# Which queue copies the kept rows of the sliding caches, and in which phases, in a four-layer decoder step

## The chip, the cores and the metric

The kernel runs on one core of one Trainium2 chip. The metric is the device time of one execution in microseconds (us). Three executions of the kernel before took 2611.56, 2619.59 and 2623.01 us; the median is 2619.59 us. The engines are TensorE (PE, with its weight loads as PEld), VectorE (DVE), ScalarE (ACT), GpSimd (POOL) and SyncE (SP), which only issues transfers. ACT and POOL can issue transfers too.

## The reference, cut to what matters

One step of a decoder runs 256 prompt tokens and 8 x 4 sample tokens through four layers: state space mixer, dilated sliding window attention, differential attention, state space mixer. Each mixer is followed by a SwiGLU network. The window layer keeps for each of 8 sequences a cache of key and value rows for three head groups (128, 512 and 1024 rows; a row has 512 floats, 2 KB). It must return each cache with the four new rows at its end:

```
keep = min(win, lb + T)
new_buf = jnp.concatenate([buf, jnp.stack([k, v], axis=2).astype(buf.dtype)], axis=1)[:, lb + T - keep:]
```

So of group 0 rows 4 to 127 are kept (124 rows, 248 KB), of group 1 rows 4 to 511 (508 rows, 1016 KB), and of group 2 all 1024 rows (2 MB), once for each of the 8 sequences. These kept rows depend on nothing that the kernel computes. They go from one tensor in device memory to another, 27.13 MB in all.

## The kernel before

Activations lie feature-major: `x` is 8 chunks of 128 features x 288 tokens. The four layers run one after the other, each as a list of phases; a phase is a block in which every engine has its own instruction list, and at its end all engines drain and meet (`L164`). An attention layer has these phases: the projection (`project`), the prompt attention, the sample attention (a loop over the 8 sequences), for the differential layer a short normalisation, and then `chain`, which holds the output projection, the gate and up projection and the down projection.

Dense layers stream their weights. SP loads a block of weights in two transfers into one of two slots `raw` (`load_block`, `L205`) once `split_lo` of the block two earlier has read the slot. ACT splits off the high part `wh` (`split_hi`, `L213`), DVE the low part `wl` (`split_lo`, `L221`), and PE runs three products per weight tile (`block_mm`, `L243` and `L248`). A down projection has 16 blocks of 128 x 1408 (384 KB and 320 KB). Two blocks make one output chunk, which DVE adds to `x` (`L440`). Then ACT, DVE and POOL prepare the chunk for the next layer: `next_act` (`L291`), `next_dve` (`L297`), `next_pool` (`L304` to `L309`). The last layer has no such preparation.

In the down projections of layers 0, 1 and 2, ACT also issues the copies of the kept rows, right behind `next_act` of each second block (`copy_rows`, `L576`): in layer 0 two for each sequence (groups 0 and 1), in layer 1 one for each sequence (the first half of group 2), in layer 2 one (the second half). That makes 32 transfers. The down projection of layer 3 has none. Nothing waits for them until the last phase, where SP waits for `copied` before the program ends.

The two prompt attention phases load no weights. SP loads the bias tables `HK` there (`sp_bias`, `L1603`: six transfers of 256 KB in the window layer, two of 768 KB in the differential layer), and later it stores the new keys and values. Before each `pe_bias` (`L1612`) PE waits for all of `HK`; its products turn the tables, ACT moves them to `BT`, and the first scores are biased with them (`L1773`, `L2200`). Everything later in the phase follows. POOL has no instruction list in these two phases.

Of the kernel before, what the change touches and what calls it, by code (L numbers as in the profile page):

```python
# [32 lines left out]
NB, T = 8, 4  # L33
# [8 lines left out]
PAST = 1024  # L42
# [16 lines left out]
HD = 64  # L59
WINDOWS = ((128, 1), (512, 4), (2048, 16))  # L60
GH = 4
# [83 lines left out]
def build_program(nc, A, O):  # L145
# [4 lines left out]
    def S(name, step=1):  # L150
        if name not in sig:
            sig[name] = Signal(nc, name, step)
        return sig[name]
# [53 lines left out]
    def split_hi(act, g, width):  # L207

        s = g % 2
        act.wait_ge(raw_loaded[s].sem, (g // 2 + 1) * 32)  # L210
        if g >= 2:
            act.wait_ge(blocks_done.sem, g - 1)
        act.activation(wts["hi"][:, s, 0:width], raw[:, s, 0:width], ACT.Copy).then_inc(hi_ready.sem, 1)  # L213
# [119 lines left out]
    def chain(layer, first, source, next_gain, nxt):  # L333
# [9 lines left out]
        with phase() as (block, sb):  # L343
# [20 lines left out]
            def width_ahead(seg, i):  # L364

                at = seg.b0 + i + 2
                for s in segs:
                    if s.b0 <= at < s.b0 + s.lin.n:
                        return s.lin.width
                return 0  # L370

            @block.sync
            def _(sp):
                for seg in segs:
                    for i in range(2 if seg is out else 0, seg.lin.n):
                        load_block(sp, seg.lin, i, seg.b0 + i)
                for i in range(2 if nxt else 0):
                    load_block(sp, nxt, i, out.b0 + total + i)

            @block.scalar  # L380
            def _(act):
                for i in range(2):
                    split_hi(act, out.b0 + i, first.width)
                for c in range(first.kk):
                    act.activation(oh[:, c, :], source(c), ACT.Copy).then_inc(src_hi.sem, src_hi.inc())
                for i in range(first.n):
                    for j in range(jj):
                        prep_act(act, i * jj + j)
                    split_hi(act, out.b0 + i + 2, width_ahead(out, i))
                rs_act(act)  # L390
                for i in range(KF):
                    split_hi(act, up.b0 + i + 2, width_ahead(up, i))
                    r = i % 2
                    act.wait_ge(gate_scaled.sem, gate_scaled.at(i + 1))
                    act.activation(sg[:, r, :], gt[:, r, :], ACT.Silu).then_inc(silu_ready.sem, silu_ready.inc())  # L395
                    act.wait_ge(gated_ready.sem, gated_ready.at(i + 1))
                    act.activation(hh[:, i, :], gh[:, r, :], ACT.Copy).then_inc(hid_hi.sem, hid_hi.inc())  # L397
                for i in range(2 * KD):
                    if i % 2 and next_gain is not None:
                        next_act(act, i // 2)  # L400
                    copy_rows(act, layer, i)
                    if width_ahead(down, i):
                        split_hi(act, down.b0 + i + 2, width_ahead(down, i))

# [152 lines left out]

    copied = S("cache_copied", 16)

    def kept_rows(layer):  # L560


        pick = lambda g, src, dst, n: (A[f"cache_swa_kv{g}"], O[f"swa_kv{g}_sample"], src, dst, n)
        return ([pick(0, T, 0, WINDOWS[0][0] - T), pick(1, T, 0, WINDOWS[1][0] - T)],
                [pick(2, 0, 0, PAST // 2)], [pick(2, PAST // 2, PAST // 2, PAST // 2)], [])[layer]

    def copy_rows(act, layer, i):

        for cache, dst, row, to, n in kept_rows(layer) if i % 2 else ():
            views = []  # L570
            for ap, at in ((cache, row), (dst, to)):
                size = ap.shape[2] * ap.shape[3] * GH * HD
                flat = ap.rearrange("l b w k h d -> (l b w k h d)")
                lo = i // 2 * size + at * 2 * GH * HD
                views.append(flat[lo:lo + n * 2 * GH * HD].rearrange("(w n) -> w n", n=2 * GH * HD))
            act.dma_start(views[1], views[0]).then_inc(copied.sem, copied.inc())  # L576

    def ffn_first(layer):
        return Linear(KF, KD, 2, gate_up(A["ffn_w_in"][layer]))
# [1059 lines left out]
    def swa(layer, nxt):  # L1639
# [11 lines left out]
        with phase() as (block, sb):  # L1651
# [9 lines left out]
            def _(sp):  # L1661
# [15 lines left out]
                        n += 1  # L1677
                sp.wait_ge(stored.sem, stored.at(n))

            def unit(u):  # L1680
                qt, hh = units[u]
                rows = slice(hh % 2 * 64, hh % 2 * 64 + 64)
                return qt, hh, rows, u % 2

            @block.tensor
            def _(pe):
# [12 lines left out]
                def scores(u):  # L1699
                    qt, hh, rows, r = unit(u)  # L1700
                    if u >= 2:
                        pe.wait_ge(sc_ready.sem, sc_ready.at(u - 1))
                    for g in range(3):
                        c = 2 * g + hh // 2
                        mm = pe.matmul(flat[:, r * 1024 + g * 256:r * 1024 + g * 256 + nk_of(qt)],
                                       X[rows, c, qt * P:(qt + 1) * P], X[rows, 6 + c, 0:nk_of(qt)],
                                       start=True, stop=True)
                    mm.then_inc(sc_done.sem, sc_done.inc())
                scores(0)
                pe.wait_ge(bias_moved.sem, bias_moved.at(6))  # L1710
                for u in range(len(units)):
                    if u + 1 < len(units):
                        scores(u + 1)
                    qt, hh, rows, r = unit(u)
                    pe.wait_ge(diag_ready.sem, diag_ready.at(2 * u + 2))
                    pe.wait_ge(p_ready.sem, p_ready.at(u + 1))
                    if u >= 1:
                        pe.wait_ge(pt_moved.sem, pt_moved.at(u))
                    for g in range(3):
                        for kt in range(qt + 1):  # L1720
                            o = 2048 + (2 * g + kt) * P
                            mm = pe.matmul(flat[:, o:o + P], Sb[:, r, g, kt * P:(kt + 1) * P], DR[:, r, :],
                                           start=True, stop=True)
                    mm.then_inc(pt_done.sem, pt_done.inc())
                    pe.wait_ge(pt_moved.sem, pt_moved.at(u + 1))
                    if u >= 2:
                        pe.wait_ge(o_moved.sem, o_moved.at(u - 1))
                    for g in range(3):
                        h = 4 * g + hh
                        for kt in range(qt + 1):  # L1730
                            mm = pe.matmul(ps[rows, 6 + r, g * P:(g + 1) * P], KV[:, kt, 1, h * HD:(h + 1) * HD],
                                           PT[:, r, 2 * g + kt, :], start=(kt == 0), stop=(kt == qt))
                    mm.then_inc(pv_done.sem, pv_done.inc())
# [322 lines left out]
    def kv_out(out):  # L2056

        return out.rearrange("l b t g m d -> (l b t) (g m d)" if len(out.shape) == 6 else
                             "l b t g n -> (l b t) (g n)")
# [13 lines left out]
    def diff(layer, nxt):  # L2073
# [13 lines left out]
        with phase() as (block, sb):  # L2087
# [7 lines left out]
            @block.sync  # L2095
            def _(sp):
                sp_bias(sp)
                sp.wait_ge(kv_moved.sem, kv_moved.at(2 * KV_C))
                for k, name in enumerate(("diff_k", "diff_v")):
                    for t in range(2):  # L2100
                        out = kv_out(O[name + "_prompt"])
                        sp.dma_start(out[t * P:(t + 1) * P], KV[:, t, k, :]).then_inc(stored.sem, stored.inc())
                    sp.dma_start(kv_out(O[name + "_sample"]), KV[0:NS, 2, k, :]).then_inc(stored.sem, stored.inc())
                sp.wait_ge(stored.sem, stored.at(6))

            def values(pe, u):
                qt, h = units[u]
                r = u % 2
                pe.wait_ge(pt_moved.sem, pt_moved.at(u + 1))
                if u >= 2:  # L2110
                    pe.wait_ge(o_moved.sem, o_moved.at(u - 1))
                for kt in range(qt + 1):
                    mm = pe.matmul(ps[:, 6 + r, 0:P], KV[:, kt, 1, h // REP * P:(h // REP + 1) * P],
                                   PT[:, r, kt * P:(kt + 1) * P], start=(kt == 0), stop=(kt == qt))
                mm.then_inc(pv_done.sem, pv_done.inc())
# [381 lines left out]
        with phase() as (block, sb):  # L2497
            act_norm, pe_norm, dve_norm, _ = norm_heads(block, sb, OT, QD_C, 0, V_DOUT, ones, P, 1.0 - LAM_INIT)
# [8 lines left out]


    kinds = (ssd, swa, diff, ssd)
    firsts = [ssd_first(0), swa_first(1), diff_first(2), ssd_first(3), None]  # L2510
    with stack:
# [85 lines left out]
```

## Time and profile before

| | |
|---|---|
| median of three executions | 2619.59 us |
| the profiled execution | 2618.41 us |
| its span, first to last instruction | 2616.6 us |
| PE busy | 2363.0 us, 90% |
| DVE, ACT, POOL busy | 1225.5, 992.4, 450.4 us |
| mean granted TensorE clock | 0.884 of full speed |

The page cuts the span into 40 slices of 65.4 us. In the lines by slices each digit is a share of a slice in tenths. The line PEclk gives the clock that was granted to TensorE, and the line DMA the mean busy share of the 16 DMA engines. A window of the trace gives the same for any stretch, in us from the span's start. A waits row names an engine's idle time by what ended it.

### The profile page before, as it was taken

The page shows a single profiled execution, that of the slowest core. Times are in us where ns is not written, and L with a number is a line of the kernel's source. Part 1 is how long each engine was busy: PE and PEld are TensorE (multiplying, and loading weights), DVE is VectorE, ACT ScalarE, POOL GpSimd, SP SyncE. Part 2 cuts the span into 40 slices and gives each one's busy share as a digit, 9 for nine tenths or more (in the row PEclk, how much of TensorE's full clock was granted, in tenths as well). Part 3 has the DMA queues.
Part 4 walks back from the last instruction along what each step waited for, and adds up shares of the span by engine and source line. Part 5 has one row for each costly group of instructions (what it writes and reads, how often), then busy time and mean ns, then how long its engine had stood idle before and what let it go on. Part 6 is the DMA issues. An engine that isn't in the chain of part 4 may idle for free. (4 is left out here: it accounts for less than half of the span.)

```text
span 2616.6 us, 38501 instructions
## 1 busy us (share of the span) xinstructions
PE 2363.0 (90%) x15187; PEld 2047.0 (78%) x15187; DVE 1225.5 (47%) x2074; ACT 992.4 (38%) x1497; POOL 450.4 (17%) x396
## 2 busy tenths in 40 slices
PE   6999997999896698999876799699988999979999
PEld 5877776999794455999874466599988877859999
DVE  5644444555433233654346433355546544445554
ACT  2534444443333111543344211444335434354442
POOL 2112120243100000442100000033310112202430
PEclk9888786999996698999995699899998878779999
DMA  5343332666750342656630445166674334225554
GB/s 159 97 118 99 101 85 73 170 167 176 258 160 23 78 113 67 177 162 200 218 113 19 170 160 194 33 174 168 182 250 133 108 100 125 75 66 159 164 152 140
DMA packets 505013, 352.44 MB, mean 135 GB/s; under 512 B 13517, under 2 KB 486367, under 8 KB 504133
## 3 DMA queue, kind: packets, MB, share of 16 engines
q1 hardware_dynamic: 503822, 323.01, 42.4%
q10 hardware_dynamic: 1024, 27.13, 2.7%
q8 instruction: 114, 1.87, 0.3%
q14 instruction: 53, 0.43, 0.1%
HBM read 326.59 MB, written 50.63 MB: 144 GB/s over the span
## 5 line engine op out<-in xcount | busy, mean ns | idle before, releaser
L243 PE MATMUL ps<-xh,wh 128*128 128x288 f32 x2368 | 676.4, 311 | 41.8 <-issue 24.9
L221 DVE TENSOR_TENSOR wl<-raw,wh 128x2048 fp32r<-128x2048 f32 (+3 forms) x241 | 503.9, 2092 | 354.7 <-ACT wh L213 350.2
L243 PE MATMUL ps<-xl,wh 128*128 128x288 f32 x2368 | 667.2, 306 | 0.0
L213 ACT ACTIVATE wh<-raw 128x2048 fp32r<-128x2048 f32 (+3 forms) x241 | 419.7, 1744 | 293.1 <-PE ps L248 183.4
L243 PEld LDWEIGHTS ps<-xh,wh 128*128 128x128 f32 x2368 | 474.9, 201 | 45.2 <-issue 41.1
L243 PEld LDWEIGHTS ps<-xl,wh 128*128 128x128 f32 x2368 | 473.8, 200 | 0.4
L248 PE MATMUL ps<-xh,wl 128*128 128x288 f32 x2368 | 340.1, 297 | 0.0
L248 PEld LDWEIGHTS ps<-xh,wl 128*128 128x128 f32 x2368 | 324.2, 189 | 0.0
L457 POOL TENSOR_TENSOR gh<-sg,ut 128x288 f32<-128x288 f32 x88 | 216.7, 2463 | 351.3 <-ACT sg L395 351.3
L243 PE MATMUL ps<-hh,wh 128*128 128x288 f32 x704 | 194.4, 301 | 17.2 <-issue 15.4
L243 PE MATMUL ps<-hl,wh 128*128 128x288 f32 x704 | 192.9, 300 | 0.0
L1466 DVE SCALAR_TENSOR_TENSOR H<-H,EA,ps 128x128 f32<-128x128 f32 x256 | 71.9, 343 | 205.2 <-PE ps L1027 205.2
L243 PE MATMUL ps<-oh,wh 128*128 128x288 f32 x400 | 114.1, 311 | 47.1 <-DVE ol L411 47.1
L1134 POOL TENSOR_TENSOR E<-E,cb 128x288 f32<-128x288 f32 x64 | 94.9, 1504 | 329.5 <-ACT E L1260 329.5
L243 PEld LDWEIGHTS ps<-hh,wh 128*128 128x128 f32 x704 | 134.2, 191 | 21.0 <-issue 17.6
L243 PEld LDWEIGHTS ps<-hl,wh 128*128 128x128 f32 x704 | 134.2, 191 | 0.0
L397 ACT ACTIVATE hh<-gh 128x288 fp32r<-128x288 f32 x88 | 39.2, 446 | 226.4 <-POOL gh L457 226.4
L243 PEld LDWEIGHTS ps<-oh,wh 128*128 128x128 f32 x400 | 80.3, 201 | 48.5 <-issue 48.5
L243 PE MATMUL ps<-ol,wh 128*128 128x288 f32 x400 | 113.3, 307 | 0.0
L291 ACT ACTIVATE xh<-x,vec 128x288 fp32r<-128x288 f32 x64 | 33.9, 535 | 201.3 <-DVE x L417 112.9
L248 PE MATMUL ps<-hh,wl 128*128 128x288 f32 x704 | 103.7, 295 | 0.0
L248 PEld LDWEIGHTS ps<-hh,wl 128*128 128x128 f32 x704 | 97.1, 189 | 0.0
(312 smaller groups left out, 3214.7 us busy)
## 6 DMA issues: line engine op xcount, KB each, us to landing
raw<-in_ffn_w_in SPq DMA_DIRECT2D x176, 512.0 KB, 5.1
raw<-in_ssm_w_in SPq DMA_DIRECT2D x80, 512.0 KB, 4.8
raw<-in_ffn_w_out SPq DMA_DIRECT2D x64, 384.0 KB, 4.8
raw<-in_ffn_w_out SPq DMA_DIRECT2D x64, 320.0 KB, 3.4
H<-in_state_ssm SPq DMA_DIRECT2D x32, 512.0 KB, 4.3
out_ssm_sample<-H SPq DMA_DIRECT2D x32, 512.0 KB, 3.2
raw<-in_ssm_w_out SPq DMA_DIRECT2D x32, 512.0 KB, 5.2
Kp<-in_cache_diff_k SPq DMA_DIRECT2D x64, 256.0 KB, 4.1
```

Source lines behind the costliest of these rows:

```text
L213: act.activation(wts["hi"][:, s, 0:width], raw[:, s, 0:width], ACT.Copy).then_inc(hi_ready.sem, 1)
L221: dve.tensor_tensor(wts["lo"][:, s, 0:width], raw[:, s, 0:width], wts["hi"][:, s, 0:width].bitcast(F32), ALU.subtract).then_inc(lo_ready.s ...
L243: pe.matmul(out, W[0][:, kk, j, :], x_[:, k, :], stop=False, start=(part == 0 and kk == 0 and x_ is seg.hi), skip_group_check=True)
L248: mm = pe.matmul(out, W[1][:, kk, j, :], seg.hi[:, k, :], start=False, stop=(part == parts - 1 and kk == lin.kk - 1), skip_group_check=True)
L291: act.activation(xh[:, c, :], x[:, c, :], ACT.Identity, scale=vec[:, 0, gain + c:gain + c + 1]).then_inc(xh_ready.sem, 1)
L397: act.activation(hh[:, i, :], gh[:, r, :], ACT.Copy).then_inc(hid_hi.sem, hid_hi.inc())
L457: pool.tensor_tensor(gh[:, r, :], sg[:, r, :], ut[:, r, :], ALU.mult).then_inc(gated_ready.sem, gated_ready.inc())
L1134: pool.tensor_tensor(E[:, h % 4, :], E[:, h % 4, :], cb[:, h // 8, :], ALU.mult).then_inc(w_ready.sem, w_ready.inc())
L1466: dve.scalar_tensor_tensor(out=H[:, c % 4, b, :], in0=H[:, c % 4, b, :], scalar=EA[:, c % 2, at:at + 1], in1=ps[:, 3, q * P:(q + 1) * P], ...
```

## The change

The call of `copy_rows` leaves the down projections. POOL gets an instruction list in both prompt attention phases, which holds nothing but the copies. In the window layer's phase it copies for each sequence the kept rows of groups 0 and 1 and the first quarter of group 2 (`PAST // 4` = 256 rows), three transfers for each sequence, 24 in all. In the differential layer's phase it copies the remaining 768 rows of group 2, one transfer for each sequence, 8 in all. The number of transfers (32) and of bytes stays the same. The wait for `copied` in the last phase stays where it was.

```
-                    copy_rows(act, layer, i)
...
-    def kept_rows(layer):
+    def kept_rows(which):
...
-        return ([pick(0, T, 0, WINDOWS[0][0] - T), pick(1, T, 0, WINDOWS[1][0] - T)],
-                [pick(2, 0, 0, PAST // 2)], [pick(2, PAST // 2, PAST // 2, PAST // 2)], [])[layer]
-
-    def copy_rows(act, layer, i):
-
-        for cache, dst, row, to, n in kept_rows(layer) if i % 2 else ():
+        return {"swa": [pick(0, T, 0, WINDOWS[0][0] - T), pick(1, T, 0, WINDOWS[1][0] - T), pick(2, 0, 0, PAST // 4)],
+                "diff": [pick(2, PAST // 4, PAST // 4, PAST - PAST // 4)]}[which]
+
+    def copy_rows(eng, which, b):
+
+        for cache, dst, row, to, n in kept_rows(which):
...
-                lo = i // 2 * size + at * 2 * GH * HD
+                lo = b * size + at * 2 * GH * HD
...
-            act.dma_start(views[1], views[0]).then_inc(copied.sem, copied.inc())
+            eng.dma_start(views[1], views[0]).then_inc(copied.sem, copied.inc())
...
+            @block.gpsimd
+            def _(pool):
+                for b in range(NB):
+                    copy_rows(pool, "swa", b)
...
+            @block.gpsimd
+            def _(pool):
+                for b in range(NB):
+                    copy_rows(pool, "diff", b)
```

## Rows read from the trace of the kernel before

**Rows 1.** The page: busy times, then PEclk and DMA by slices.

```profile
PE 2363.0 (90%) x15187; PEld 2047.0 (78%) x15187; DVE 1225.5 (47%) x2074; ACT 992.4 (38%) x1497; POOL 450.4 (17%) x396
...
PEclk9888786999996698999995699899998878779999
DMA  5343332666750342656630445166674334225554
```

**Rows 2.** Windows: first to last addition to x in the four down projections, then two prompt phases.

```profile
core 0: us, PE busy (x) PEld busy (x) DVE busy (x) ACT busy (x) POOL busy (x), PEclk, DMA share, GB/s
639.40:710.50 71.10, 64.20 (x463) 61.76 (x461) 27.91 (x28) 21.68 (x20) 10.65 (x13) 1.00 0.82 265
1206.10:1279.00 72.90, 65.77 (x462) 64.50 (x461) 27.63 (x28) 21.69 (x20) 10.88 (x13) 0.95 0.74 236
1877.00:1942.60 65.60, 62.32 (x462) 61.48 (x460) 27.67 (x27) 21.71 (x20) 10.89 (x13) 1.00 0.81 260
2547.40:2609.10 61.70, 61.70 (x462) 61.47 (x460) 24.30 (x20) 17.97 (x13) 0.00 (x0) 1.00 0.50 141
...
777.00:881.00 104.00, 66.85 (x300) 54.10 (x300) 34.62 (x73) 32.86 (x45) 0.29 (x1) 0.64 0.10 30
...
1351.00:1460.00 109.00, 70.48 (x308) 50.67 (x308) 68.60 (x192) 58.94 (x146) 0.00 (x0) 0.60 0.09 26
```

**Rows 3.** Waits in these down projections, in order of layers 0, 1, 2 and 3.

```profile
ACT wh L213 <- DMA raw<-in_ffn_w_out: 26.9, 9, 5.6
...
ACT wh L213 <- DMA raw<-in_ffn_w_out: 26.2, 6, 6.3
...
ACT wh L213 <- DMA raw<-in_ffn_w_out: 19.0, 6, 5.0
...
ACT wh L213 <- PE ps L248: 39.3, 13, 3.0
```

**Rows 4.** DVE's timeline in layer 1: the first five of eight additions to x.

```profile
1206.12 0.46 DVE L440 TENSOR_TENSOR x<-x,ps 128x288 f32<-128x288 f32 x1 [1.29 <-PE ps L248]
1214.94 0.45 DVE L440 TENSOR_TENSOR x<-x,ps 128x288 f32<-128x288 f32 x1 [1.31 <-PE ps L248]
1223.76 0.45 DVE L440 TENSOR_TENSOR x<-x,ps 128x288 f32<-128x288 f32 x1 [1.31 <-PE ps L248]
1236.66 0.45 DVE L440 TENSOR_TENSOR x<-x,ps 128x288 f32<-128x288 f32 x1
1248.17 0.45 DVE L440 TENSOR_TENSOR x<-x,ps 128x288 f32<-128x288 f32 x1
```

**Rows 5.** One line, L576: the copies, by layer (duration ns min/median/max, first and last start).

```profile
L576 ACTq DMA_DIRECT2D out_swa_kv_sample<-in_cache_swa_kv x16: 517/602/642, 639.9 to 711.5; - x16
...
L576 ACTq DMA_DIRECT2D out_swa_kv_sample<-in_cache_swa_kv x8: 517/518/537, 1206.6 to 1279.5; - x8
```

**Rows 6.** The copies' queue (packets, MB, share), one kind of copy, L205's landing (layers 0, 3).

```profile
q10 hardware_dynamic: 1024, 27.13, 2.7%
...
out_swa_kv_sample<-in_cache_swa_kv ACTq DMA_DIRECT2D x8, 1016.0 KB, 7.8
...
DMA to landing us min/median/max: 3.3/5.3/8.8
...
DMA to landing us min/median/max: 3.3/4.1/4.6
```

**Rows 7.** HK's transfers by phase (issue), and the time to landing of each phase's.

```profile
L1603 SPq DMA_DIRECT2D HK<-dist_tab x6: 366/503/824, 777.2 to 779.8; - x6
...
DMA to landing us min/median/max: 3.4/4.7/5.8
...
L1603 SPq DMA_DIRECT2D HK<-dist_tab x2: 371/567/763, 1351.1 to 1351.5; - x2
...
DMA to landing us min/median/max: 6.4/7.7/9.0
```

**Rows 8.** PE's timeline where HK is first read, in the window and the differential layer.

```profile
804.97 1.28 PE L1612 MATMUL ps<-cst,HK 128*128 128x128 f32 x10
...
1382.70 1.00 PE L1612 MATMUL ps<-cst,HK 128*128 128x128 f32 x7
```

**Rows 9.** What GpSimd waits for around the prompt phases, and its first work after the window's.

```profile
POOL Qall L1831 <- POOLq L164: 167.9, 1, 167.9
...
L1831 POOL MEMSET Qall<- x1: 737/737/737, 880.7 to 880.7; 128x768 f32 x1
```

## The prediction

> **What bounds the kernel now.** I read the page first. PE is busy for 90% of the span, DVE for 47%, ACT for 38%, and the DMA engines reach their highest shares in some slices in which PE is just short of full [rows 1]. So PE's work is the bound, and a change of order can only win where PE stands idle or runs at the lower of its two clocks (1.2 instead of 2.4 GHz).
>
> Second come windows around the phases that lose the copies, from the first to the last addition to `x`. Each holds the same 14 weight blocks [rows 2]. Layers 0, 1 and 2 take 71.10, 72.90 and 65.60 us. Layer 3, which has no copies, takes 61.70 us, and PE has no idle time in it. The DMA share is 0.74 to 0.82 in the first three and 0.50 in the last. Third, the waits inside the windows name the cause [rows 3]: in the first three ACT waits 26.9, 26.2 and 19.0 us for the weights of this projection, in the last it waits for nothing but PE. Fourth, DVE's timeline of layer 1 shows how it builds up [rows 4]: the additions are 8.82 us apart twice, then 12.90 and 11.51. The two slots of `raw` have no reserve. A late load makes `split_hi`, `split_lo` and the next load late.
>
> The landings agree [rows 6]: the median load takes 5.3 us and the longest 8.8 us in layer 0, against 4.1 and 4.6 us in layer 3.
>
> **The change, part by part.**
>
> *The copies leave the down projections.* If these windows become as long as layer 3's, the gain is 71.10 + 72.90 + 65.60 - 3 x 61.70 = 24.5 us. The lowest figure that the same rows allow is PE's idle time alone, 6.90 + 7.13 + 3.28 = 17.3 us; the rest is PE's own work made longer, in layer 1 by a clock of 0.95, which is full speed with stretches at the lower level, after PE had stood idle. Layer 3 has no preparation of a next layer, so it could be too good a measure. But layer 1's first two pairs, which have this preparation and the issue of a copy, take 8.82 us [rows 4], and layer 3's average is 61.70 / 7 = 8.81 us. So the preparation costs nothing, and I take 24.5 us.
>
> *ACT's issues.* 16 at 0.602 and 16 at 0.518 us [rows 5] are 17.9 us of ACT's queue. They lie in front of `split_hi`, but ACT is busy for only 21.7 of some 70 us there [rows 2]. Beyond the waits already counted I give them nothing. If that cover were gone they would be inside the 24.5 us anyway.
>
> *POOL's issues.* There are 24 in the window layer and 8 in the differential layer. POOL has 0.29 us of work in the first of these phases and none in the second [rows 2], and its next instruction starts at 880.7 us [rows 9]. Nothing is queued behind the copies but POOL's drain at the phase's end. No row shows a transfer issued by POOL. The near end is ACT's 0.6 us, so 24 x 0.6 = 14 us. The far end is the point at which the phase gets longer, 104 / 24 = 4.3 us each. Anything below costs nothing. I take that, nearer to ACT's row.
>
> The Trainium skill, DMA: Bandwidth & Descriptors, Specifications, puts the first byte at about 1 us through GpSimd and 0.6 us through the hardware queues; by that estimate the sum would be the same, and no trace here shows GpSimd's.
>
> *The data.* The copies' packets took 2.7% of 16 engines' span, 0.027 x 2616.6 = 70.6 us if all engines move them at once [rows 6]. The window phase gets 8 x 1776 KB = 14.55 MB of the 27.13 MB, so 37.9 us; the differential phase gets 12.58 MB, 32.7 us. These phases last 104 and 109 us with a DMA share of 0.10 and 0.09 [rows 2], so all of it fits.
>
> *What it may collide with.* At the start of both phases SP loads `HK`, now together with the copies. In the window layer the last `HK` transfer is issued at 779.8 and lands by 785.6 us at the latest [rows 7]; PE reads `HK` first at 804.97 [rows 8], a slack of 19.4 us. In the differential layer it is 1360.5 against 1382.70, a slack of 22.2 us. Behind that PE waits for `HK`, ACT for PE's products, DVE for `BT`, and all scores for DVE, so what exceeds the slack lengthens the phase in full. The low end is no delay. The high end is that `HK` gets an engine only after all copies: 785.6 + 37.9 - 804.97 = 18.5 us and 1360.5 + 32.7 - 1382.70 = 10.5 us, together 29.0 us. The nearest row is the weight landings of layer 0: two copies issued together held a load for at most 8.8 - 4.6 = 4.2 us [rows 6], which the slack would swallow. But there at most two stand behind one another, here up to 24, so I don't take the bare low end. I allow the time of one 1016 KB copy in each phase, 70.6 x 1.04 / 27.13 = 2.7 us, 5.4 us in all.
>
> A rule of the Trainium skill speaks against this change here (DMA: Bandwidth & Descriptors, Queues, rings and completion order): each engine takes turns between its queues packet by packet, some 9 to 17 descriptors to a packet. By it, as an estimate, the window layer's `HK` (six transfers of 256 KB over 16 engines, 192 rows of 512 bytes for each) is 11 to 21 turns, each behind one copy's piece of 37.9 / 24 = 1.6 us; that is 18 to 34 us of delay, none to 14 us past the slack. The sum would then be a gain of 10 to 24 us. No row here shows which turns are taken with many copies in line.
>
> *The sum.* -24.5 + 5.4 = -19.1 us. Against the profiled execution's 2618.41 us that is 2599.3; the median of the runs is 1.2 us above it, so **2600 us**. No change within 0.5%, 13 us, can be told by this measurement.
>
> **The rivals.**
>
> *HK comes late.* The copies keep the engines and `HK` lands after PE wants it. For it: a copy's pieces are large, and 24 transfers can be in line before `HK` is through. Against: slacks of 19.4 and 22.2 us, and that POOL must first issue them. With the whole 29.0 us the time is 2619.6 - 24.5 + 29.0 = 2624; with half of it 2610. The gain would have been moved, not made.
>
> *The down projections stay late.* Their own loads, 5 us in a ring of two slots, would keep ACT waiting without copies too. Against it stand layer 3 without one such wait [rows 3] and layer 1's first pairs. If half of the 24.5 stays, the time is 2619.6 - 12.3 + 5.4 = 2613.
>
> *POOL is slow (slower than before).* If one issue on POOL takes over 4.3 us, its drain ends the window phase. At 6 us, 24 issues last 144 us instead of 104, which is 40 us more, while the 8 of the differential phase still fit (48 of 109 us). The time is 2619.6 - 24.5 + 40 = 2635. The kernel gets slower than before from 24.5 / 24 = 1.0 us above the 4.3, at 5.3 us for an issue. Against it: ACT issues the same kind in 0.52 to 0.60 us [rows 5]. For it: only that no row shows POOL doing it, and that it waits 167.9 us without work here [rows 9], so nobody has seen what it would do.
>
> **How the numbers follow.** Forecast 0.47, with a range of its own of 2594 to 2607; `HK` late 0.30, of which 0.10 still beats 0.5%; down projections still late 0.10; POOL slow 0.08; other 0.05. The lower end is the full 24.5 us with no delay of `HK`, 2595, and 3 us for the projections behind the down projections, which start while the last copy is in flight. The upper end takes in nearly the whole delay of `HK`. That gives 2592 to 2622. Faster by over 0.5%: nearly all of the forecast, 0.10 of the `HK` case and little else, 0.55. Slower by over 0.5%: POOL slow and a rest, 0.09. Within: 0.36.
>
> **What would show it.** The windows of layers 0 to 2 from first to last addition should be 61.5 to 63 us with PEclk 1.00, and ACT's wait for the weights there near zero. The three weights' landings should read like layer 3's, 4.1 us. PE's first read of `HK` should stand 28 us behind the start of the window phase and 31.6 behind that of the differential phase; more than 31 and 35 proves the first rival, and a wait of PE for `HK` by name would appear. POOL's issues should end well before the phase. The prediction is wrong if the first windows stay near 70 us, or if the prompt phases grow by over 10 us together.

## The result and the profile after

The changed kernel takes 2652.36 us (median of four runs, 2650.33 to 2655.23), against 2621.3 us (median of four) before. The ratio is 1.012, with a 95% interval of 1.0082 to 1.0159: slower, where I had forecast a gain of 19 us. The profiled span is 2648.5 us in place of 2616.6.

First the windows of the trace after. Four of them hold the down projections from first to last addition to `x`. The last two hold the two prompt attention phases from their first transfer to GpSimd's first work of the next phase. The columns are those of [rows 2].

```profile
639.80:701.60 61.80, 61.75 (x463) 61.52 (x461) 28.27 (x28) 20.95 (x20) 10.66 (x13) 1.00 0.61 175
1226.20:1288.00 61.80, 61.75 (x463) 61.52 (x461) 27.95 (x28) 20.95 (x20) 10.89 (x13) 1.00 0.60 174
1906.90:1968.60 61.70, 61.69 (x462) 61.45 (x460) 27.91 (x27) 20.96 (x20) 10.89 (x13) 1.00 0.57 166
2579.30:2641.00 61.70, 61.69 (x462) 61.45 (x460) 24.28 (x20) 17.97 (x13) 0.00 (x0) 1.00 0.49 141
767.80:898.00 130.20, 68.75 (x300) 55.73 (x300) 34.55 (x72) 32.87 (x45) 11.70 (x25) 0.62 0.41 136
1361.00:1489.40 128.40, 72.49 (x308) 52.22 (x308) 68.44 (x193) 58.86 (x146) 3.94 (x8) 0.59 0.37 120
```

The down projections of layers 0 to 2 are as short as layer 3's, 61.8, 61.8 and 61.7 us, with PE busy throughout. That is the forecast gain: 71.1 + 72.9 + 65.6 - 185.3 = 24.3 us. It is lost again in the two prompt phases. The window layer's took 103.5 us before (from the first `HK` transfer at 777.2 to 880.7, [rows 7, 9]) and takes 130.2 us now. The differential layer's took 109.7 us (1351.1 to GpSimd's first work at 1460.8) and takes 128.5 us (1360.9 to 1489.4). Together these are 45.5 us more.

The waits of the two phases name the cause. PE, which never waited for `HK` before, now does:

```profile
PEld ps L1610 <- DMA HK<-dist_tab: 25.1, 1, 25.1
PE ps L1610 <- DMA HK<-dist_tab: 24.8, 1, 24.8
...
PEld ps L1610 <- DMA HK<-dist_tab: 17.9, 1, 17.9
PE ps L1610 <- DMA HK<-dist_tab: 17.6, 1, 17.6
```

The next lines show the transfers: for each phase `HK`'s issue (ns min/median/max, first and last start) and its time to landing (us min/median/max), then GpSimd's issues in the window phase. They answer to [rows 7] and [rows 5].

```profile
L1601 SPq DMA_DIRECT2D HK<-dist_tab x6: 366/504/10087, 767.8 to 770.6; - x6
...
DMA to landing us min/median/max: 3.5/34.0/49.7
...
L1601 SPq DMA_DIRECT2D HK<-dist_tab x2: 370/566/762, 1360.9 to 1361.3; - x2
...
DMA to landing us min/median/max: 9.5/28.6/47.7
...
L574 POOL DMA_DIRECT2D out_swa_kv_sample<-in_cache_swa_kv x24: 486/486/677, 768.3 to 779.5; - x24
```

`HK` landed within 5.8 and 9.0 us before and now takes up to 49.7 and 47.7 us. GpSimd isn't slow: 0.486 us for an issue, less than ACT's 0.52 to 0.60. All 24 copies are in line 12 us after the phase's start. PE's first product with `HK` now stands 52.5 and 48.1 us behind the two phases' starts, in place of 27.8 and 31.6. One of SP's issues of `HK` took 10 us itself.

Windows inside the window phase show what the engines did meanwhile:

```profile
780.00:800.00 20.00, 6.30 (x36) 4.98 (x36) 9.72 (x27) 7.66 (x7) 0.00 (x0) 0.67 0.99 319
800.00:812.00 12.00, 0.00 (x0) 0.00 (x0) 0.00 (x0) 0.00 (x0) 0.00 (x0) 0.50 0.97 311
```

The DMA engines are full and from 800 to 812 us no compute engine works at all. PE's clock stands at 0.50, its level of 1.2 GHz, after PE had been idle.

The copies' queue, to be set beside [rows 6]:

```profile
q0 software_dynamic: 1152, 27.13, 3.0%
```

The copies' packets take 3.0% of 16 engines' span, 79.5 us of all engines, where I had reckoned with 70.6.

The two terms, 24.3 us gained and 45.5 us lost, give +21.2 us of the 31.9 us between the profiled spans. Of the other 10.7 us, 5.9 lie between the last addition of layer 2 and the last of layer 3 (666.5 us before, 672.4 after), where both kernels do the same work with no copy in flight, but for the last copy of layer 2 in the kernel before (until 1949.0). In the eight experiments below, this stretch took between 657.4 and 672.4 us, 665.4 in the one without any copies, so I take it for spread from run to run and not for an effect of the change. The remaining 4.8 us are scattered in pieces of up to 2.8 us and are not explained.

### The profile page after: what moved, and what is told of

Read it like the earlier page. It is cut to its first block and busy times, and to the rows that moved or that the text cites. A ratio compares the mean times of both kernels' runs of the same rounds, so it can differ in the third digit from the quotient of the medians.

```text
span 2648.5 us, 38501 instructions
## 1 busy us (share of the span) xinstructions
PE 2374.6 (90%) x15187; PEld 2054.5 (78%) x15187; DVE 1228.6 (46%) x2074; ACT 990.5 (37%) x1497; POOL 446.2 (17%) x428
## 3 DMA queue, kind: packets, MB, share of 16 engines
q0 software_dynamic: 1152, 27.13, 3.0%
## 5 line engine op out<-in xcount | busy, mean ns | idle before, releaser
L243 PE MATMUL ps<-oh,wh 128*128 128x288 f32 x400 | 114.8, 313 | 47.7 <-DVE ol L410 47.7
L1132 POOL TENSOR_TENSOR E<-E,cb 128x288 f32<-128x288 f32 x64 | 75.1, 1193 | 327.8 <-ACT E L1258 327.8
```

Of the source, the lines that this page charges most:

```text
L243: pe.matmul(out, W[0][:, kk, j, :], x_[:, k, :], stop=False, start=(part == 0 and kk == 0 and x_ is seg.hi), skip_group_check=True)
L1132: pool.tensor_tensor(E[:, h % 4, :], E[:, h % 4, :], cb[:, h // 8, :], ALU.mult).then_inc(w_ready.sem, w_ready.inc())
```

## The experiments

Theory A: the copies' large pieces keep the DMA engines from `HK`, PE waits for it, and nothing else of weight goes wrong. The rivals: GpSimd's queue or the extra traffic costs time wherever it stands in the phase (B), or any copies at the phase's start do, in whatever queue (C). The kernel before was timed on the same chips: 2618.64 us beside the first four experiments, 2619.69 us beside the others.

**Copies after HK.**

```
             def _(pool):
+                pool.wait_ge(hankel_in.sem, hankel_in.at(6))
                 for b in range(NB):
                     copy_rows(pool, "swa", b)
...
+                pool.wait_ge(hankel_in.sem, hankel_in.at(2))
```

> The changed kernel, but GpSimd waits in each prompt phase until all of HK has landed, and only then issues its copies. Theory A (the copies keep the engines from HK): PE's wait for HK, 24.8 and 17.6 us in the changed kernel, is gone, both prompt phases are again 104 and 109 us long, the down projections keep 61.8 us each, and the whole is 2621 - 24 = 2597 us, or up to 2608 us if the 10.6 us by which the changed kernel is slower outside the down projections and the prompt phases stay. Rival B (GpSimd's queue or the traffic beside the attention costs time wherever it stands in the phase): the phases stay above 120 us and the whole above 2640 us.

Measured: 2600.93 us, ratio to before 0.9937 (0.9913 to 0.9962). A down projection and the two prompt phases in windows, then `HK` in the window and the differential layer:

```profile
635.00:696.70 61.70, 61.66 (x462) 61.43 (x460) 28.23 (x28) 20.95 (x20) 10.65 (x13) 1.00 0.60 175
762.80:865.70 102.90, 66.19 (x300) 53.53 (x300) 34.56 (x72) 32.87 (x45) 11.69 (x25) 0.65 0.52 172
1328.60:1437.10 108.50, 69.96 (x308) 49.95 (x308) 68.59 (x193) 58.96 (x146) 3.97 (x9) 0.61 0.44 142
```

```profile
DMA to landing us min/median/max: 3.4/4.4/5.1
...
DMA to landing us min/median/max: 6.3/7.6/8.9
```

The wait for `HK` is gone and both phases are as long as before, although the same 27.13 MB move in them, at a DMA share of 0.52 and 0.44. B falls: beside the rest of the phase the queue and the traffic cost nothing that can be told.

**Small pieces.** Each engine's contiguous stretch of a copy becomes rows of 512 bytes that are 8 KB apart.

```
-                views.append(flat[lo:lo + n * 2 * GH * HD].rearrange("(w n) -> w n", n=2 * GH * HD))
+                views.append(flat[lo:lo + n * 2 * GH * HD].rearrange("(q p n) -> p q n", p=16, n=P))
```

> The changed kernel with every copy written as pieces of 512 bytes, the size of HK's own rows, in place of up to 64 KB; same bytes, same queue, same start. If the engines take turns between the queues one piece at a time, HK now gets half of them and lands within 20 us of the phase's start, before PE asks for it at 28 us; the prompt phases are again near 104 and 109 us and the whole is near 2600 us, if GpSimd can issue so many pieces in time. If turns are by transfer or by order of issue, the size of a piece changes nothing: PE waits 20 us or more for HK and the whole stays near 2650 us. The copies themselves should take longer in all, some 90 us of all engines in place of 80.

Measured: 2599.37 us, ratio 0.995 (0.9915 to 0.9985; the quotient of the two medians, 0.9926, lies within). PE didn't wait for `HK`, and the two phases took 103.1 and 110.0 us. The copies' queue on the page, `HK`'s landing in the window and the differential layer:

```profile
q0 software_dynamic: 7168, 27.13, 3.2%
```

```profile
DMA to landing us min/median/max: 3.4/9.2/24.5
...
DMA to landing us min/median/max: 7.5/17.5/27.4
```

The copies start as early as in the changed kernel, and `HK` still lands just in time, within 27.4 us of its issue. Of the 7168 packets, 512 only count a completion (16 for each of 32 transfers). So a packet carries 27.13 MB / 6656 = 4.1 KB: GpSimd's queue packs eight rows into one. The copies took 83 us of all engines (3.2% of the span), less than the expected 90. The expected landing of 20 us was missed in both layers, since a turn of the copies is 4 KB and not 512 bytes.

The whole alone doesn't show what the size of a piece is worth, because a second thing changed with it. GpSimd's issues, in the window and the differential layer:

```profile
767.71 10.47 POOL L574 DMA_DIRECT2D out_swa_kv_sample<-in_cache_swa_kv  x13 [64.38 <-POOLq L164]
799.87 9.05 POOL L574 DMA_DIRECT2D out_swa_kv_sample<-in_cache_swa_kv  x11 [21.69 <-issue]
...
1330.40 6.49 POOL L574 DMA_DIRECT2D out_swa_kv_sample<-in_cache_swa_kv  x5 [70.75 <-POOLq L164]
1366.18 3.88 POOL L574 DMA_DIRECT2D out_swa_kv_sample<-in_cache_swa_kv  x3 [29.29 <-issue]
```

GpSimd stopped after 13 of 24 and 5 of 8 copies, and went on only after `HK` had landed. So 7.5 and 7.9 MB stood in line against `HK`, not 14.55 and 12.58. Large pieces with that line would by the changed kernel's rate have let `HK` land 8.4 + 42.8 x 7.5 / 14.55 = 30.5 us after the window phase's start and 9.4 + 36.8 x 7.9 / 12.58 = 32.5 us after the other's. This is an estimate: 8.4 and 9.4 us are `HK`'s own times to its last landing before [rows 7], 42.8 and 36.8 us what the copies took of all engines in the changed kernel's two phases. PE would have waited some 3 and 2 us. In fact `HK`'s last rows came after 26.5 and 27.2 us, when 6.0 MB of the copies had moved in each phase. So `HK` did overtake the line, by some 4 and 5 us, but most of the time that this kernel wins back may come from the shorter line.

What a turn is doesn't hang on that. It can be counted from the trace's records of single packets, while both queues had work:

```
kernel, stretch (us)           HK's rows of 512 B    copies' packets (data + completions)
changed kernel, 778 to 810     502                   260 + 260
changed kernel, 1373 to 1398   242                   163 + 80
small pieces, 778 to 788       805                   743 + 85
```

In each stretch `HK` gets one row for one packet of the copies, whatever its size. With the completions of `HK`'s own queue, 16, none and 20, its side comes to 518, 242 and 825 against 520, 243 and 828. With data pieces of 16 to 64 KB and rows of 512 bytes, that is next to nothing: in the changed kernel 606 and 634 of the 3072 rows of `HK` came only after the copies' last packet.

**No copies.** `copy_rows` issues nothing, and GpSimd has no lists in the two phases. So this kernel leaves the kept rows out and is only a bound.

> The changed kernel without any copy of the kept rows: those rows of three outputs are left unwritten. It is the ceiling: every wait that copies cause is gone. Theory A: 2621 - 24 = 2597 us. If the changed kernel's 10.6 us outside the down projections and the prompt phases come from the copies too, nothing of them is seen here; if they come from how the stretches at the lower clock fall, part of them may remain, up to 2608 us.

Measured: 2597.53 us, ratio 0.9919 (0.9889 to 0.995). By their medians the kernels with the copies behind `HK` and in small pieces are 3.4 and 1.8 us above it, which their intervals don't tell apart.

**Copies in SP's queue, behind HK.**

```
                 sp_bias(sp)
+                for b in range(NB):
+                    copy_rows(sp, "swa", b)
                 sp.wait_ge(kv_moved.sem, kv_moved.at(24))
```

and the same with "diff" in the other phase, without GpSimd's lists.

> The changed kernel with the copies issued by SP in the same two phases, right behind HK's transfers, so in the same queue and in order behind them. Theory A: HK is through before the first copy, PE doesn't wait for it, and the whole is 2597 to 2608 us. The stores of new keys and values now stand behind the copies, but a phase of 104 us has room for 43 us of copies. Rival C (any 14.5 MB of copies at the phase's start delay it, in whatever queue): PE waits for HK as in the changed kernel, above 15 us in each phase, and the whole is above 2635 us.

Measured: 2598.07 us, ratio 0.9931 (0.9907 to 0.9956). `HK`'s landing in the window and the differential layer:

```profile
DMA to landing us min/median/max: 3.4/4.4/6.7
...
DMA to landing us min/median/max: 6.2/8.7/11.1
```

C falls: as many bytes from the start of the phase cost nothing if they stand behind `HK` in its own queue.

**GpSimd's queue in the down projections.** The kernel before with one change:

```
-                    copy_rows(act, layer, i)
...
                 for c in range(KD if next_gain is not None else 0):
                     next_pool(pool, c)
+                    copy_rows(pool, layer, 2 * c + 1)
```

> The kernel before with one thing changed: in the down projections of layers 0 to 2 GpSimd issues the copies, behind its preparation of each chunk, where ACT did. Same transfers, same phases. If what a copy costs there is the engines' time (weights held back by pieces of 64 KB), the windows from first to last addition stay at 66 to 73 us where 61.8 is the undisturbed time, and the whole stays at 2619 us, within 8 us. If ACT's 18 us of issuing was the cost, the windows fall to 62 us and the whole to 2597 us.

Measured: 2621.65 us, ratio 1.0014 (0.9975 to 1.0052).

```profile
634.80:700.90 66.10, 63.02 (x462) 61.62 (x461) 28.33 (x27) 21.61 (x20) 17.57 (x27) 1.00 0.89 288
1208.30:1273.40 65.10, 62.52 (x462) 61.59 (x461) 27.95 (x28) 21.60 (x20) 14.25 (x20) 1.00 0.87 270
1878.00:1943.30 65.30, 62.65 (x462) 61.49 (x460) 27.83 (x28) 21.61 (x20) 14.25 (x20) 1.00 0.84 262
```

The whole is unchanged, as expected. The windows are not: 66.1, 65.1 and 65.3 us are 13.1 us shorter together than [rows 2], though 11.2 us longer than undisturbed. The whole doesn't show it, because the time is lost right behind the windows. ACT's first wait in the phase behind layer 0's down projection, before and in this kernel:

```profile
ACT wh L213 <- PEq L164: 1.9, 1, 1.9
...
ACT wh L213 <- PEq L164: 8.1, 1, 8.1
```

Behind layers 1 and 2 it is 7.7 and 7.0 us, where it was 1.7 and 1.7: together 17.5 us more at the ends of three phases. In this kernel the next phase starts 1.0 to 1.3 us after the last packet of the copies in each layer (708.7, 1281.1 and 1950.2 us against 710.0, 1282.1 and 1951.2). In the kernel before, where ACT issues, the next phase starts at 713.4 us while the copies run on to 718.4. The likely reading is that GpSimd's drain at a phase's end waits for the transfers that GpSimd issued, and ACT's doesn't; no run separates the two. So the experiment leaves 11.2 of the 24.3 us to the engines' time and doesn't rule out that ACT's issues, or when they come, cost the other 13.1.

**The wait in one phase only.** The wait for `HK` stands in the window layer alone.

> The changed kernel with GpSimd's wait for HK in the window layer's phase only; the differential layer's copies start at once, as in the changed kernel. Theory A: PE waits for HK only in the differential layer, 17 to 18 us; the window phase takes 103 us and the differential phase 128 us; the whole is that of the kernel with both waits and 19 us more, 2601 + 19 = 2620 us, no different from the kernel before. If the two phases' delays are not independent, the whole is clearly elsewhere.

Measured: 2614.83 us, ratio 0.9974 (0.9951 to 0.9997). PE's wait for `HK` in the whole trace:

```profile
PE ps L1610 <- DMA HK<-dist_tab: 19.0, 1, 19.0
```

One wait, in the differential layer, of 19.0 us. The window phase takes 102.7 us and the differential phase 129.2, as expected. The whole is 14 us over the kernel with both waits by the medians, and 10 us by the two ratios, instead of 19; the width of the intervals allows that. Each phase pays for its own copies.

**Five sequences ahead.**

```
                 for b in range(NB):
+                    if b == 5:
+                        pool.wait_ge(hankel_in.sem, hankel_in.at(6))
                     copy_rows(pool, "swa", b)
```

with the wait ahead of all copies in the differential layer.

> The changed kernel, but in the window layer GpSimd issues the copies of only five of the eight sequences at the start and waits for HK before the other three; in the differential layer it waits before the first. If HK lands when the copies in line are through, it lands 5 x 42.6 / 8 + 8.4 = 35 us after the phase's start, PE asks for it at 28 us and waits 7 us in place of 24.8; the window phase takes 110 to 112 us and the whole 2601 + 8 = 2609 us. If any unpaced start of the copies costs all of the delay, PE waits 20 us or more; if the queues share fairly with this many, it doesn't wait.

Measured: 2617.1 us, ratio 0.9972 (0.9937 to 1.0008). The window layer:

```profile
PE ps L1610 <- DMA HK<-dist_tab: 10.1, 1, 10.1
...
L1601 SPq DMA_DIRECT2D HK<-dist_tab x6: 366/504/14210, 765.0 to 767.8; - x6
...
DMA to landing us min/median/max: 3.5/26.3/33.8
```

PE waits 10.1 us, between 24.8 with eight sequences ahead and nothing with none; I had 7. The direction and the size of the model hold: `HK` lands when the copies in line are through. The window phase takes 114.4 us, somewhat over the 110 to 112. The whole is 8 us above the expected 2609, and its interval touches no change. In its profile the stretch from the window layer's sample phase to layer 1's first addition took 343.3 us (879.4 to 1222.7), where the first four experiments and the one before this took 325 to 328 us, with the same work and no copies in it. The windows of that stretch, here and in the experiment before:

```profile
879.40:1222.70 343.30, 323.08 (x2054) 246.13 (x2055) 148.29 (x257) 97.10 (x116) 71.83 (x49) 0.87 0.46 125
...
864.00:1192.30 328.30, 308.54 (x2054) 240.98 (x2055) 148.33 (x256) 97.11 (x116) 71.80 (x49) 0.91 0.47 131
```

PE's own busy time makes 14.5 of the 15.0 us, at a granted clock of 0.87 in place of 0.91. The last experiment shows the same without being made for it, 339.8 us at 0.87. So it isn't `HK`; why the clock was lower is open.

**ACT's hardware queue at the phase's start.** ACT issues the copies ahead of its other work:

```
+                for b in range(NB):
+                    copy_rows(act, "swa", b)
                 act_norm(act)
```

> The changed kernel with the copies issued by ACT at the start of the two phases, before its other work, so in a hardware queue of their own and not GpSimd's software queue. If it is the turn by piece between any two queues that starves HK, HK's median landing is near 34 and 29 us again, as in the changed kernel. If it is a trait of GpSimd's queue, HK lands within 10 us. ACT's own work starts 12 us and more later in both phases, so the whole is not comparable; what is read is HK's landing and PE's wait.

Measured: 2664.42 us in a single execution. The kinds of transfer, KB each and the median us to landing:

```profile
HK<-dist_tab SPq DMA_DIRECT2D x6, 256.0 KB, 43.8
HK<-dist_tab SPq DMA_DIRECT2D x2, 768.0 KB, 46.9
```

`HK` starves in the same way, and somewhat more, for a reason that I didn't trace. The counts are the same too: from 780 to 810 us `HK`'s queue has 493 rows and 10 completions beside 251 data packets and 251 completions of ACT's. PE's waits for it are smaller, 9.4 and 11.7 us, since ACT's own work is late too. So it isn't a trait of GpSimd's software queue: ACT's hardware queue with the same large pieces does it too.

## Why the prediction was wrong

**What bounds, and the gain in the down projections: right.** I had 24.5 us; the windows give 24.3. Their PEclk is 1.00, ACT waits for weights there only once (3.1 us, in layer 2), and the measure from layer 3 held for layers with a next layer's preparation.

**POOL's issues at nothing: right.** GpSimd needs 0.486 us for each of the 24 in the window phase, all 32 are done long before the phases end, and the slow-POOL rival didn't occur. **ACT's issues at nothing: not shown.** With GpSimd as the issuer the three windows were 13.1 us shorter, so part of the 24.3 us may hang on ACT's queue. The sum doesn't change by it, since the prediction had said that such a part would lie inside the 24.5 us.

**The step that failed is the delay of HK.** I had placed it rightly, had the chain behind it and the slack (19.4 and 22.2 us), and then took 2.7 us in each phase because at most two copies had held a single weight load for 4.2 us. The prediction named that difference, at most two copies there and up to 24 here, and drew almost nothing from it. With one row of `HK` for one packet of a copy, a load of 192 rows on each engine meets 48 packets of the window phase's copies there (24 pieces, 24 completions) and gets through only when the line is empty. Measured is the high end and more: PE waits of 24.8 and 17.6 us in place of 5.4 together. The sum with my own upper bound, 2624 us, was already outside the range that I gave.

**The high end itself was too low**, 29.0 us where the phases grew by 45.5. The copies took 79.5 us of all engines and not 70.6, which is 8.9 us more over both phases. The waits together, 42.4 us, leave 3.1 us of growth; the bias products behind the wait, run partly at the lower clock, are part of it, 7.0 us (820.3 to 827.3) where the kernel with both waits takes 5.4 (790.4 to 795.8). Of the remaining 4.5 us between 29.0 + 8.9 and 42.4, 1.1 is that PE asks earlier in the differential layer, 30.5 us after the phase's start in place of 31.6. The other 3.4 I can't divide. The copies' packets run from 770.8 to 818.4 and from 1366.5 to 1406.4 us; that is 87.5 us, of which they keep the engines busy for 79.6, with `HK`'s rows and gaps between them.

**The rule that I weighed**, turns by packets of 9 to 17 descriptors (the Trainium skill, DMA: Bandwidth & Descriptors, Queues, rings and completion order), pointed the right way. By it the window layer's `HK` would be at most 14 us late; the trace shows 24.8, and its counts show turns of one 512-byte descriptor for SP's hardware queue. Turns by packet agree, the size of a packet doesn't.

**The rival "HK comes late" was the outcome**, at 0.30 of the chances, with a time of 2610 to 2624 that was too mild. That it would cross into slower was in none of my cases; it needs the two phases' loss to exceed 24.3 + 13 us, which 45.5 does.

## What to carry to other kernels

A transfer that has an idle DMA stretch to itself on average can still starve a small one that is due in the first quarter of it. Compare the landing that the critical load needs with the whole backlog of the other queue and not with a single transfer of it: with large contiguous pieces against 512-byte rows, the load lands when the backlog is empty. Put bulk copies behind the critical load, by a wait or in the same queue; then moving them out of the weight-bound phases is worth 0.6 to 0.7% here (ratios 0.9937 and 0.9931), and the kernel without copies gains no more that can be told (0.9919). And if GpSimd issues them, don't do it late in a phase: the phase ended only when they had landed.

## What the runs showed of the hardware that I had not expected

The DMA engines served two busy queues one packet for one packet, without regard to bytes: 502 rows of 512 bytes beside 520 packets of the copies in one stretch, 805 beside 828 in another where the copies' data packets were 4 KB. A completion of 4 bytes counts for a turn like a piece of 64 KB. Smaller pieces cost the copies only 3.2% in place of 3.0% of the engines' span, and let `HK` land while copies still stood in line; the fall of its longest landing from 49.7 to 24.5 us in the window layer owes much to GpSimd's pause of 21.7 us, whose cause isn't shown. With a backlog in a second queue, issuing becomes slow as well: single issues of `HK` by SP took 10.1 us in the changed kernel, 14.2 us with five sequences ahead and 30.9 us beside ACT's queue, against 0.8 at most before [rows 7]. Copies issued by GpSimd late in a phase held the next phase back until they had landed, 7.0 to 8.1 us of ACT's time where ACT's own copies left 1.7 to 1.9.
